# Second and third key tile in upper and lower parts; a block matrix zeroed and filled later; a scratch matrix in another home; the last doubling of the turns on VectorE

## What is computed

```python
z = x @ w_in[i]
u_pool, q, k, v, u_ssm = jnp.split(z, splits, axis=-1)
y_pool = pool_mixer(u_pool, w_pool[i], pool_scale[i])          # trailing means of windows 2, 4, 8, 16
y_attn = chunk_attention(q, k, v, rel_bias[i])                 # 6 heads of 64, causal by chunk
y_ssm = s5_mixer(u_ssm, ...)                                   # 24 groups, complex diagonal scan
heads = jnp.concatenate([rms_norm(y_pool, ...), rms_norm(y_attn, ...), rms_norm(y_ssm, ...)], axis=-1)
h = layer_norm(DN_ALPHA * x + heads @ w_out[i], ...)
```

```python
_, _, s_re, s_im = lax.associative_scan(_complex_affine_combine, elems, axis=1)
y = jax.nn.gelu(y.reshape(bsz, l, SSM_WIDTH)).astype(u.dtype)
return y * jax.nn.sigmoid(y @ w_glu + b_glu)
```

## Time and profile before

| what | value |
|---|---|
| median of 3 runs | 423.56 us (422.49 to 425.38) |
| profiled execution, own time | 422.09 us |
| its span, first to last instruction | 420.3 us |
| TensorE busy | 407.8 us (97%) |
| VectorE busy | 260.9 us (62%) |
| ScalarE busy | 143.8 us (34%) |
| GpSimd busy | 115.5 us (27%) |
| chain that ended last | TensorE 47%, VectorE 29%, issue 11%, DMA 5%, GpSimd 4%, ScalarE 3% |

### The profile page before, as it was taken

One profiled execution on the slowest core, in us unless ns is written; L12 is line 12 of the kernel. 1 busy time (PEld: TensorE's weight loads), 2 busy tenths in 40 slices (PEclk: granted clock), 3 DMA queues, 4 the chain that ended last, 5 costly groups with the idle time before them and its releaser, 6 DMA issues.

```text
span 420.3 us, 5727 instructions
## 1 busy us (share of the span) xinstructions
PE 407.8 (97%) x2213; PEld 246.0 (59%) x2213; DVE 260.9 (62%) x467; ACT 143.8 (34%) x254; POOL 115.5 (27%) x142
## 2 busy tenths in 40 slices
PE   8999999999999999999999999999999999999992
PEld 5767755459987557888587876333333333333281
DVE  2999994999884999999988323111110112224986
ACT  4732236248757891214520101011111011111284
POOL 2811258457054706000001640011101111000050
PEclk9999999999999999999999999999999999999998
DMA  7994103350579995111763239999999999978204
GB/s 269 430 403 139 50 2 62 74 131 27 132 294 343 397 409 202 50 51 50 271 281 105 95 85 387 423 394 423 420 419 419 417 412 409 423 279 299 101 13 188
DMA packets 33643, 102.77 MB, mean 245 GB/s; under 512 B 14898, under 2 KB 16098, under 8 KB 26832
## 3 DMA queue, kind: packets, MB, share of 16 engines
q1 hardware_dynamic: 26048, 92.79, 56.8%
q0 software_dynamic: 4016, 7.97, 5.6%
q10 hardware_dynamic: 3552, 1.65, 1.4%
HBM read 93.29 MB, written 15.24 MB: 258 GB/s over the span
## 4 chain that ended last, share of the span: by engine, by line
PE 47%; DVE 29%; issue 11%; DMA 5%; POOL 4%; ACT 3%; SPq 0%; DVEq 0%; POOLq 0%; ACTq 0%
PE bank L1392 20%; PE bank L1402 10%; DVE region_f L1812 4%; PE bank L1387 3%; PE bank L1227 3%; PE bank L1467 3%; PE bank L1143 2%; POOL slot_scratch L631 1%; DMA region_h<-y_scratch 1%; ACT region_a L767 1%; DVE ln_st L1815 1%; DVE region_a L1658 1%; DVE region_a L1676 1%; DVE att_mx L1667 1%; DMA region_h<-slot_scratch 1%
## 5 line engine op out<-in xcount | busy, mean ns | idle before, releaser
L1392 PE MATMUL bank<-region_a,region_g 128*64 128x512 f32 (+1 forms) x224 | 77.8, 594 | 0.0
L1974 DVE TENSOR_TENSOR region_c<-region_c,bank 128x256 f32<-128x256 f32 x12 | 5.1, 421 | 64.7 <-ACT region_c L962 64.7
L1402 PE MATMUL bank<-region_a,region_c 128*64 128x512 f32 (+1 forms) x160 | 43.7, 596 | 0.0
L1392 PE MATMUL bank<-region_h,region_g 128*64 128x512 f32 (+1 forms) x96 | 42.4, 594 | 0.0
L1392 PE MATMUL bank<-region_c,region_g 128*32 128x512 f32 (+1 forms) x96 | 42.4, 595 | 0.0
L1392 PE MATMUL bank<-region_b,region_g 128*64 128x512 f32 (+1 forms) x96 | 42.4, 594 | 0.0
L1967 DVE COPY region_g<-bank 128x512 f32<-128x512 f32 x24 | 15.4, 686 | 40.6 <-PE bank L1387 40.6
L1392 PEld LDWEIGHTS bank<-region_a,region_g 128*64 128x64 f32 (+1 forms) x224 | 22.2, 123 | 25.1 <-issue 24.4
L962 ACT ACTIVATE region_c<-bank 128x256 f32<-128x256 f32 x12 | 4.6, 384 | 83.9 <-PE bank L1392 83.9
L1013 PE MATMUL bank<-region_e,region_a 128*128 128x512 f32 x64 | 28.0, 595 | 0.0
L1320 PE MATMUL bank<-ple_gate_upper,hidden_upper 128*128 128x512 f32 x64 | 25.7, 402 | 0.0
(11 more groups left out here) (380 smaller groups left out, 969.8 us busy)
## 6 DMA issues: line engine op xcount, KB each, us to landing
region_a<-in_w_exp_down SPq DMA_DIRECT2D x10, 1024.0 KB, 11.9
region_a<-in_w_exp_gate SPq DMA_DIRECT2D x7, 1024.0 KB
region_a<-in_w_exp_up SPq DMA_DIRECT2D x7, 1024.0 KB
expert_scratch<-zero_scratch SPq DMA_DIRECT2D x8, 512.0 KB, 13.7
region_b<-in_w_out SPq DMA_DIRECT2D x1, 3072.0 KB, 12.4
region_c<-in_w_ple_gate SPq DMA_DIRECT2D x2, 1536.0 KB, 12.0
region_b<-in_w_exp_gate SPq DMA_DIRECT2D x3, 1024.0 KB, 10.1
region_b<-in_w_exp_up SPq DMA_DIRECT2D x3, 1024.0 KB, 11.7
```

Source lines behind the costliest of these rows:

```text
L1392: return mm(out_[at:at + width].rearrange("p (u n) -> p u n", u=2), x[:, k, at:at + width], w[:, k], start=(k == 0), stop=(k == KD - 1), t ...
L1402: return mm(bank[banks[half]][at:at + width, :], act_e[:, r, 2, k * P + at:k * P + at + width], w[:, k, half * 512:half * 512 + 512], star ...
```

## The change

The second and third key tile go through `qk_split`, with an upper part of their weights of their own (`kn_hi`, 128x1536, in region_h behind column 6144, made by ScalarE behind the bxT copies) and a lower part in the rest of `kw_lo` (made by VectorE behind the row maxima). So `ux_hi` and `ux_lo` live until `pe_qk` is 6. For that, `bxT` moves to region_a. `m0` is no longer zeroed by GpSimd: GpSimd makes a tile of zeros (128x1024, region_c, where bx was), SyncE sends `zero_scratch` from it, and ScalarE copies it three times onto `m0` behind its copy of the third key tile. The block moves of SyncE and GpSimd wait for these copies (`kern_done` 5), and the load of rcnt for `pe_qk` 6. GpSimd stops doubling at m = 16; VectorE does m = 32. GpSimd's first sums wait for `p_norm` 2 (normalisation of head 1) and its multiplication by rcnt for `glu_lo_set` 4 (the last lower gelu part).

```diff
-        bxT = RC[:, 3072:6144].rearrange("p (r q s) -> p r q s", r=2, q=Q)
+        bxT = RA[:, 2560:5632].rearrange("p (r q s) -> p r q s", r=2, q=Q)
...
+        kn_hi = over("next_key_upper", 6 * 2 * P, H0 + 4 * 6144)
+        zero = RC[:, 768:768 + D]
...
@@ SyncE @@
-            sp.wait_ge(S["rot_ready"], 2)
-            sp.dma_start(zero_d, RH[:, 3072:3072 + D]).then_inc(S["ye_zero"], 16)
-            sp.wait_ge(S["ye_zero"], 16)
-            sp.wait_ge(S["kern_done"], 2)
+            sp.wait_ge(S["rot_ready"], 3)
+            sp.dma_start(zero_d, zero).then_inc(S["ye_zero"], 16)
+            sp.wait_ge(S["kern_done"], 5)
...
-            sp.wait_ge(S["pe_x"], 1)
+            sp.wait_ge(S["pe_qk"], 6)
             load(rcnt, io["rcnt"], "rc_in")
@@ GpSimd @@
-            while m < NC:
+            while m < NC // 2:
...
-                    gp.wait_ge(S["pe_qk"], 4)
-                    g.memset(m0, 0.0).then_inc(S["rot_ready"], 1)
...
+            gp.wait_ge(S["pe_bxT"], 6)
+            g.memset(zero, 0.0).then_inc(S["rot_ready"], 1)
             gp.wait_ge(S["rot_ready"], 3)
             gp.wait_ge(S["gp_in"], 16 * 4)
-            gp.wait_ge(S["ye_zero"], 16)
-            gp.wait_ge(S["kern_done"], 2)
+            gp.wait_ge(S["kern_done"], 5)
...
             gp.wait_ge(S["pe_x"], 1)
+            gp.wait_ge(S["p_norm"], 2)
...
             gp.wait_ge(S["rc_in"], 16)
+            gp.wait_ge(S["glu_lo_set"], 4)
             link(g.tensor_tensor(a, a, rcnt, ALU.mult))
@@ ScalarE @@
+            ac.wait_ge(S["pe_qk"], 4)
+            a.activation(kn_hi[:].rearrange("p (k n) -> p k n", k=6), w_k[:, 2:KD, P:ATT_W], ACT.Copy).then_inc(S["xw_hi_set"], 1)
...
             qk_copy(4)
             qk_copy(5)
+            ac.wait_ge(S["rot_ready"], 3)
+            for i in range(3):
+                a.activation(RH[:, 3072 + i * D:3072 + (i + 1) * D], zero, ACT.Copy).then_inc(S["kern_done"], 1)
...
             ac.wait_ge(S["wv_in"], 32)
+            ac.wait_ge(S["ye_zero"], 16)
+            ac.wait_ge(S["kern_done"], 5)
@@ TensorE @@
             pe.wait_ge(S["kern_done"], 1)
-            qk(4)
+            qk_split(4, w_k, kn_hi, kw_lo, 2 * P, 11)
             pe.wait_ge(S["kern_done"], 2)
-            qk(5)
+            qk_split(5, w_k, kn_hi, kw_lo, 2 * P, 11)
@@ VectorE @@
-            dv.wait_ge(S["pe_x"], 1)
-            dv.wait_ge(S["rot_ready"], 3)
+            dv.wait_ge(S["xw_hi_set"], 11)
+            tt(kw_lo[:].rearrange("p (k n) -> p k n", k=6)[:, :, P:ATT_W], w_k[:, 2:KD, P:ATT_W],
+               kn_hi[:].rearrange("p (k n) -> p k n", k=6), ALU.subtract).then_inc(S["xw_lo_set"], 1)
+            dv.wait_ge(S["rot_ready"], 2)
...
+            wide_ = [P, Q, NC // 2]
+            turn_r, turn_i = rot[:, 0], rot[:, 1]
+            at_r, at_i = (t_[:, :, NC // 2:NC // 2 + 1].broadcast_to(wide_) for t_ in (turn_r, turn_i))
+            cmul(turn_r[:, :, NC // 2 + 1:NC + 1], turn_i[:, :, NC // 2 + 1:NC + 1], turn_r[:, :, 1:NC // 2 + 1], turn_i[:, :, 1:NC // 2 + 1],
+                 at_r, at_i, x_tmp[:, 0, 0:Q * NC // 2].rearrange("p (q c) -> p q c", q=Q))
+            dv.wait_ge(S["pe_x"], 1)
```

More of the change, by code:

```diff
@@ L589, in _ @@
             add_shift(b2, a, 2, 64, slice(0, 1))
-            gp.wait_ge(S["xw_hi_set"], 14)
+            gp.wait_ge(S["xw_hi_set"], 15)
             gp.wait_ge(S["pe_v"], 1)
@@ L1052, in qk_split @@
                     for k in range(6):
-                        mm(dst, w_hi[:, k * width + m * P:k * width + (m + 1) * P], x[:, k * T:(k + 1) * T], start=False, stop=False)
+                        c = k * width + (m * P if n < 4 else (m - 1) * P)
+                        mm(dst, w_hi[:, c:c + P], x[:, k * T:(k + 1) * T], start=False, stop=False)
                 pe.wait_ge(S["xw_lo_set"], parts)
@@ L1069, in upper @@
                     return homes[i][:, first:first + w]
-                for term, (signal, count) in enumerate((("xw_hi_set", 14), ("gp_lo_set", 2), ("xw_lo_set", 12))):
+                for term, (signal, count) in enumerate((("xw_hi_set", 15), ("gp_lo_set", 2), ("xw_lo_set", 13))):
                     pe.wait_ge(S[signal], count)
@@ L1733, in _ @@
             row_max(5)
-            dv.wait_ge(S["xw_hi_set"], 12)
+            dv.wait_ge(S["xw_hi_set"], 13)
             dv.wait_ge(S["pe_v"], 1)
```

## The result

| | before | after |
|---|---|---|
| median | 423.56 us (422.49 to 425.38) | 440.1 us (439.15 to 440.39) |
| ratio, 95% interval | | 1.0386 (1.0359 to 1.0412) |
| span of the profiled execution | 420.3 us | 438.4 us |
| mean granted clock | 0.996 | 0.962 |
| TensorE busy | 407.8 us | 418.5 us |

What follows compares the result with a forecast made beforehand. Bound: the wait chain from w_glu's load through ScalarE's exponentials and y to TensorE's turn at 120.26 us. Queue 6.2 later plus 0.4 behind rcnt, less a 0.84 wait, gives 5.8: 423.56 becomes 429.4 us, range 426 to 432.

Steps and rivals of the forecast that it cites:

- the sign: Whole kernel: slower by 5.8 us, with a chance of 0.77 for slower.
- the queue: SyncE's DMA queue: late block moves hold back the state moves and the load of w_glu by 6.2 us.
- The term behind rcnt: SyncE's queue: state moves wait behind the load of rcnt; between 0 and 2.4 us, taken as 0.4.
- The 1.2 us: SyncE's queue: estimated time of rcnt's 512 KB at 436 GB/s, which would make the sum 6.6 instead of 5.8.
- Its 2.2 us are spent waiting: TensorE: the 2.2 us saved on two key tiles go into waits before the y products and before 126.1.
- Rival B: TensorE's new waits: the clock falls, costing 0 to 5.6 us, taken as 2, giving 431.4 us; chance 0.12.
- Behind the first: Matmuls after TensorE's wait of about 5.2 us ahead of the y products: slowness covered, since TensorE waits again.
- the second wait: TensorE before the turn of head 3, at about 126: a wait of 4 us, slow matmuls behind it on the path.
- Rival C: SyncE's queue is not in the way and the chain gains; 421.7 us, faster by 0.4%; chance 0.03.
- Rival A: Same mechanism, smaller: quicker block-move issue, no wait behind rcnt, cheaper zero copies; delay 3.8 us, 427.4 us; chance 0.13.
- Rival D: Key tiles in parts aren't ready or bring nothing, so zeros and queue come 2.2 us later; 431.6 us; chance 0.04.
- The parts costed at nothing: Upper and lower key weights on ScalarE and VectorE, and GpSimd's wait for glu_lo_set: each priced at zero.

Runs made afterwards that it cites:

- e2_state_first: Changed kernel, SyncE's queue reordered: 8 block moves, state moves, w_glu, then the other 8 block moves and rcnt; 437.4 us, ratio 1.0293.
- e3_spread: Changed kernel, state moves and w_glu behind SyncE's first 8 block moves, 4 of the other 8 issued by ScalarE; 436.66 us, ratio 1.0279.
- e1_fill_wait: Changed kernel with seven unused 512-column float32 matmuls added in TensorE's wait ahead of the y products; 428.04 us, ratio 1.0086.
- e4_keys_full: Changed kernel with second and third key tile in full float32 again, without their lower weights on VectorE; 438.65 us, ratio 1.0322.
- e8_before_dve: Kernel before with only the last doubling on VectorE and GpSimd's first sums behind the second normalisation; 421.35 us, ratio 0.9927.
- e11_three_parts: e8_before_dve plus GpSimd's multiplication by rcnt behind the last lower gelu part; 420.09 us, ratio 0.9904.
- e6_before_wait: Kernel before with one added wait: TensorE starts the y products only after the exponentials of head 3; 438.57 us, ratio 1.0337.
- e9_dve_wait_h3: e8_before_dve with TensorE's added wait for the exponentials of head 3 ahead of the y products; 434.87 us, ratio 1.0246.
- e7_spread_fill: e3_spread with four added 512-column float32 matmuls in TensorE's wait ahead of the y products; 424.45 us, ratio 1.0008.
- e10_dve_wait_h2: e8_before_dve with TensorE's added wait for the exponentials of head 2; three of four executions 430.88 to 431.98 us, one 422.70.

## Why the prediction was wrong

**Right: where it happens, the sign, and the queue.** By its own steps: key tiles 5.9 us each (5.84 said), zero copies done at 79.7 (80.1), block moves from 79.7 (80), state ready at 84.6 (84.5), state moves at 90.84 (91.75), w_glu at 101.6 (101.1), TensorE free ahead of the y products at 93.6 (93.5), and its wait 6.1 us (5.2). Issuing the 16 moves took 10.43 instead of 11.02 us. The term behind rcnt, taken as 0.4, is not measured alone: the state moves took 5.21 us to issue instead of 3.67 and w_glu landed 5.5 us after its issue, 0.2 more than before. What was under-sized is the landing of the state moves: their median was 5.7 us instead of 4.0, so that the y products began at 99.75 where 98.7 was said. But in e2_state_first and e3_spread, where rcnt goes out last, the median was 5.4 and 5.7 us too, so rcnt ahead of them does not explain it. The 1.2 us that the prediction named beside it rest on a fit that the Trainium skill (DMA: Bandwidth & Descriptors, "Anatomy of one DMA — SWDGE (gpsimd) path") gives for DMAs issued by GpSimd, while SyncE issues rcnt. In e1_fill_wait, with the clock kept, these steps give the last copy of y to within 0.5 us (113.68, forecast 114.2). From there the way out to y_scratch and back was 1 us shorter: D u starts at 121.77, 4.3 us later than before, where 5.8 was said.

**The step that failed** is the sentence "TensorE, though it begins the y products only at 98.7, is done with them 107.32 - 96.65 = 10.7 us later, at 109.4, before that." It sized the products at full clock. They took 20.5 us, and with them the last copy of y and the value tile were late. Kept at full clock, they make the kernel 12.1 us faster (e1_fill_wait). From this came the wrong claim that "Its 2.2 us are spent waiting".

**Rival B was the right mechanism and had the wrong place and price.** It had the wait, and a row that bore on it (the clock fell behind the only long gap). It then reasoned that "Behind the first, slow matmuls are covered, since TensorE waits again anyway", and put the price behind the second wait at 2 us. The cover was 114.2 - 109.4 = 4.8 us; doubling 10.7 us of work needs 10.7. The sum was never made. The second wait was also mis-added: behind the y products TensorE had 12.2 us of work up to the turn (107.32 to 119.52), so by the prediction's own terms it would have waited 126.1 - 109.4 - 12.2 = 4.5 us, not 4, and was not "a little shorter" than the 4.5 us of the earlier trace rows. I also took for granted that the clock would be back soon once TensorE worked again, which no row of the kernel before showed, since it had no such gap. A bound from the rows at hand (the y products at half speed from 98.7 to 120.1, then the 12.2 us of work with 4.3 more for the value tile at half speed) would have put the turn at 136.6 instead of 126.1: 10.5 us more than the forecast, about 440. And "The short earlier waits of the kernel never cost the clock" was true of the one profile but carried little: 1.6 us ahead of the same matmuls cost it in three of four executions, and the kernel before itself lost it somewhere in two of its executions.
The Trainium skill (TensorE: Matmul & The Clock Gate, "HAM oscillation — how this bites in real kernels") had the rule that spoke against this change, and I cited it; the trace agrees that gaps bring the clock down. Its section "What's actually happening" has activity release the throttle; here TensorE was busy the whole 20.5 us and nothing was released until the value tile; the measurement decides.

**Rival C was refuted as an outcome, not as a wish:** e2_state_first and e3_spread show that getting the state and w_glu out early is possible, and that the blocks are then late. The queue can be shifted but not emptied: 32 moves that start at 80 us are in the way of somebody. **Rival A** had its first term right (10.43 us of issuing, 0.6 less), the zero copies were no cheaper (2.94 us for three), and it is without weight beside 12 us. **Rival D** is refuted by the key tiles and by e4_keys_full. The parts costed at nothing were indeed free, and two of them are gains that the change hid: the doubling and the two waits of GpSimd (e8_before_dve, e11_three_parts). I had valued the wait for `glu_lo_set` at zero, which is right where TensorE waits elsewhere. Between these two runs it is worth 1.3 us by the medians and 0.7 us with each run held against its own set; the wait that it removed was 0.8 us.

What stays open: why the wait for the gathered rows is 0.4 to 0.6 us in some versions and 1.5 to 2.3 us in others (2.3 in after, 2.1 in e2_state_first and e3_spread, 0.5 in e4_keys_full), and with it some 2 to 3 of the 16.5 us. Each is one profiled execution, and no run aimed at it. The executions of the kernel before lie for the most part near 423 us or near 425 us, the slower ones at a slightly lower mean clock (down to 0.989), and its profile is of a quick one (422.09 us, 0.996). A wait that is sometimes short and sometimes long would fit that, but it is not shown: no trace of an execution near 425 us is kept. Open is also what wait is borne where: 2.0 us before the turn of head 3 in e1_fill_wait, ahead of matmuls of 128 and then 384 columns, cost nothing; 1.6 us before the 64-column ones did, and so did 2.3 us at the gathered rows in after, ahead of matmuls of 128 and then 512 columns. That the light matmuls behind a wait count with it is an idea that no run tested by changing only them.

## What to carry to other kernels

A new wait of TensorE is not priced by its length: price everything behind it, up to the next wide matmuls, at half clock, and compare that sum with the cover. This holds above all ahead of a stretch of narrow matmuls, which here neither brought the clock back in 20.5 us nor, with 1.6 us of waiting before them, kept it in three of four executions. And a change of several parts is better tried part by part: the doubling and the two waits of GpSimd were worth 1% together, and the key tiles in parts, with the late filling of a matrix that they ask for, turned that into a loss of 4%.

## What the runs showed that I had not expected

- 64-column matmuls at 100% busy ran at 0.50 for over 20 us (after, e6_before_wait, e9_dve_wait_h3), and at 1.00, in 10.7 us, with no wait to speak of ahead of them (e1_fill_wait, e7_spread_fill, e8_before_dve).
- Four 512-column matmuls ahead of them, useless in themselves, made the changed kernel 8.3 us faster by the medians (440.1 to 431.78), even behind the wait; seven inside it, 12.1 us.
- The clock fell up to 2.3 us after a wait was over (e10_dve_wait_h2), in some executions of a kernel and not in others.
- The kernel before, with no wait above 1 us near the y products in its profile, took some 11 us longer in 2 of 41 executions, at a mean clock of 0.965.
- GpSimd and VectorE slowed each other: with GpSimd's 128x1024 operations beside them three lower gelu operations took 6.56 us, and 2.06 without; GpSimd's own operation took 2.73 and 2.37 us.
